# Two blocks of a transformer on one core: the parts of the latent projection in two banks, and two weight splits in other places

## What is computed

```python
h = rms_norm(x, norm_mix_pre[i])
z = h @ w_in[i]
c_q, c_kv, k_rope, q_c, k_c, v_c, g_a, g_b, g_c = jnp.split(z, split_points, axis=-1)
o_a = mla_attention(c_q, c_kv, k_rope, ...)      # latent attention, 8 heads
o_b = fourier_mix(h)
o_c = windowed_gqa(q_c, k_c, v_c, ...)           # 8 heads
merged = (jax.nn.sigmoid(g_a) * (o_a @ w_branch_a[i]) + jax.nn.sigmoid(g_b) * (o_b @ w_branch_b[i])
          + jax.nn.sigmoid(g_c) * (o_c @ w_branch_c[i]))
x = x + rms_norm(merged @ w_out[i], norm_mix_post[i])
h = rms_norm(x, norm_ffn_pre[i])
ff = (jax.nn.silu(h @ w_ffn_gate[i]) * (h @ w_ffn_up[i])) @ w_ffn_down[i]
x = x + rms_norm(ff, norm_ffn_post[i])
e = (p[i] @ w_ple_proj[i]) * jax.nn.sigmoid(x @ w_ple_gate[i])
x = x + rms_norm(e, norm_ple[i])
```

## Time and profile before

| | |
|---|---|
| median of 3 runs | 1958.55 us (1958.01 to 1962.77) |
| the profiled execution | 1960.33 us |
| its span in the trace | 1958.5 us |
| PE busy | 1895.8 us, 97% of the span |
| DVE, ACT, POOL busy | 57%, 49%, 9% |
| place A | 15 to 46 us |
| place B | 478 to 514 us |
| place C | 945 to 970 us |

### The profile page before, as it was taken

The page is one execution under the profiler, slowest core; times in us unless marked ns, Lnnn a source line. Parts: engine busy times, 40 slices in busy tenths (PEclk is TensorE's granted clock), DMA queues, the critical chain, the costliest instruction groups (busy, mean ns, idle before and its releaser), DMA issues.

```text
span 1958.5 us, 26222 instructions
## 1 busy us (share of the span) xinstructions
PE 1895.8 (97%) x9054; PEld 1544.7 (79%) x9054; DVE 1112.5 (57%) x1340; ACT 958.2 (49%) x1256; POOL 169.5 (9%) x262
## 2 busy tenths in 40 slices
PE   8999999999999999999999999899999999989998
PEld 7777888887876888888788887688888888758886
DVE  6565664458566565455744455654565445555544
ACT  5555454445556445444544445544455444555443
POOL 5310010000321001000100012000011000100000
PEclk9999999999999999999999999999999999999999
DMA  6234555554423556555555553365555555435552
GB/s 219 97 110 155 193 193 193 193 193 153 162 65 129 181 175 221 182 184 189 188 184 192 193 185 127 109 209 193 193 187 179 193 193 175 160 107 172 185 183 104
DMA packets 204843, 332.71 MB, mean 170 GB/s; under 512 B 11344, under 2 KB 150224, under 8 KB 204752
## 3 DMA queue, kind: packets, MB, share of 16 engines
q1 hardware_dynamic: 200240, 319.33, 48.3%
q0 software_dynamic: 3120, 11.02, 1.7%
q10 hardware_dynamic: 1392, 1.21, 0.2%
HBM read 330.47 MB, written 1.05 MB: 169 GB/s over the span
## 4 chain that ended last, share of the span: by engine, by line
PE 84%; issue 6%; ACT 4%; DVE 3%; POOL 1%; DMA 1%; ACTq 0%; DVEq 0%; POOLq 0%
PE ps L542 26%; PE ps L554 26%; PE ps L549 26%; PE ps L576 3%; ACT whi L1207 2%; PE ps L720 1%; PE ps L732 1%; PE ps L748 1%; ACT prob L1304 1%; DVE soft L1786 0%; DVE wlo L1659 0%; DMA freq<-freq_dram 0%; DVE prob L1798 0%; DMA gains<-gains_dram 0%; DVE prob L1779 0%
## 5 line engine op out<-in xcount | busy, mean ns | idle before, releaser
L1659 DVE TENSOR_TENSOR wlo<-raw,whi 128x2048 fp32r<-128x2048 f32 (+1 forms) x304 | 686.1, 2257 | 543.0 <-ACT whi L1207 542.5
L1207 ACT ACTIVATE whi<-raw 128x2048 fp32r<-128x2048 f32 (+2 forms) x308 | 581.0, 1886 | 427.4 <-PE ps L554 425.3
L542 PE MATMUL ps<-whi,act_hi 128*128 128x512 f32 (+1 forms) x1632 | 444.7, 393 | 5.4 <-issue 2.1
L549 PE MATMUL ps<-wlo,act_hi 128*128 128x512 f32 (+1 forms) x1632 | 442.3, 389 | 0.0
L554 PE MATMUL ps<-whi,act_lo 128*128 128x512 f32 (+1 forms) x1632 | 435.7, 388 | 0.7 <-DVE act_lo L1665 0.7
L554 PEld LDWEIGHTS ps<-whi,act_lo 128*128 128x128 f32 x1632 | 304.9, 188 | 65.0 <-DVE act_lo L1665 1.6
L549 PEld LDWEIGHTS ps<-wlo,act_hi 128*128 128x128 f32 x1632 | 303.2, 188 | 63.2 <-issue 1.1
L542 PEld LDWEIGHTS ps<-whi,act_hi 128*128 128x128 f32 x1632 | 298.1, 188 | 64.5 <-issue 2.9
L1251 ACT ACTIVATE hid<-ps,stat 128x256 f32<-128x256 f32 x132 | 62.7, 475 | 282.9 <-PE ps L576 197.3
L2214 POOL TENSOR_TENSOR stat<-stat,eps 128x1 f32<-128x1 f32 x44 | 23.0, 522 | 1494.1 <-ACT prob L1238 1493.8
L1711 DVE SCALAR_TENSOR_TENSOR hid<-ps,stat,hid 128x256 f32<-128x256 f32 x132 | 63.5, 481 | 123.1 <-ACT hid L1251 123.1
(11 more groups left out here) (203 smaller groups left out, 1652.4 us busy)
## 6 DMA issues: line engine op xcount, KB each, us to landing
raw<-ffn_w_gate_dram SPq DMA_DIRECT2D x88, 512.0 KB, 4.0
raw<-ffn_w_up_dram SPq DMA_DIRECT2D x88, 512.0 KB, 5.0
raw<-ffn_w_down_dram SPq DMA_DIRECT2D x88, 512.0 KB, 3.9
raw<-w_in_dram SPq DMA_DIRECT2D x64, 512.0 KB, 4.3
raw<-w_ffn_gate_dram SPq DMA_DIRECT2D x44, 512.0 KB, 4.0
raw<-w_ffn_up_dram SPq DMA_DIRECT2D x44, 512.0 KB, 5.0
raw<-w_ffn_down_dram SPq DMA_DIRECT2D x44, 512.0 KB, 3.9
raw<-a_w_qkv_dram SPq DMA_DIRECT2D x24, 512.0 KB, 4.4
```

The costliest lines, as they stand in the source:

```text
L542: nc.tensor.matmul(o, hi, a, start=start and i == 0, stop=False)
L549: nc.tensor.matmul(o, hi, a, start=False, stop=False)
L1207: nc.scalar.activation(whi[:, u % SLOTS, 0:words], raw[:, u % SLOTS, 0:words], ACT.Copy)\
L1659: nc.vector.tensor_tensor(wlo[:, u % SLOTS, 0:words], raw[:, u % SLOTS, 0:words], whi[:, u % SLOTS, 0:words].bitcast(F32), ALU.subtract)\
```

## The change

1. PE's parts of the latent projection take turns in two banks: parts 0 and 2 of tile t in bank 4 + 2t, part 1 in bank 5 + 2t. Part 1 waits for no reader any more, part 2 for the reader of part 0. DVE reads from the bank that belongs to the part.
2. At a layer's end DVE splits unit 2 of the next layer ahead of tile 1's residual (`add_embedded(13, 1)`), not behind it.
3. ACT splits unit 3 at the head of the next layer, ahead of `square_second`, not at the end of the layer before. On the way from the first to the second layer this is the same order with the loop's return ahead of the split. At the second block's start the split comes behind the first `silu` and ahead of `square_second`. At the start of the program it moves into the loop.

```diff
@@ PE, layer1 @@
-                        free_before("half", HF_Z + 2 * c + t)
+                        if c == 0:
+                            free_before("half", HF_Z + t)
+                        elif c == 2:
+                            was_read("half", HF_Z + t)
...
-                                                [([ps[:, 4 + 2 * t, 0:cols]], act_hi[:, 4 * j + k, t * P:(t + 1) * P],
+                                                [([ps[:, 4 + 2 * t + c % 2, 0:cols]], act_hi[:, 4 * j + k, t * P:(t + 1) * P],
@@ ACT, ffn @@
                 silu(gu, 0)
-                if between is None:
-                    split(1)
-                else:
+                split(1)
+                if between is not None:
                     between()
@@ ACT, ahead of the loop @@
             split(1)
             at_start = False
-            split(1)
...
-                done[0] = SLOTS + 1
+                done[0] = SLOTS
@@ DVE, z_half @@
-                    nc.vector.tensor_scalar(zs[:, t, n0:n0 + cols], half_bank(hf)[:, 0:cols], scale_of(w, t), None,
-                                            ALU.mult)\
+                    nc.vector.tensor_scalar(zs[:, t, n0:n0 + cols], half_bank(hf, 2)[:, c % 2 * 512:c % 2 * 512 + cols],
+                                            scale_of(w, t), None, ALU.mult)\
```

More of the change, by code:

```diff
@@ L1512, in _ @@
             at_start = False
-            split(1)
             with act.Fori(0, DEPTH) as li:
                 w.layer = li
-                done[0] = SLOTS + 1
+                done[0] = SLOTS
                 layer1()
-                assert done[0] == UNITS1 + SLOTS + 1, done
+                assert done[0] == UNITS1 + SLOTS, done
             w.layer = None
-            done[0] = SLOTS + 1
+            done[0] = SLOTS
             sq, tn, hf, gu, hv = T, 0, 0, 0, 0
```

## The result

| | before | changed |
|---|---|---|
| median of 20 runs each, us | 1959.6 (1957.09 to 1964.16) | 1963.24 (1958.77 to 1967.22) |
| ratio, 95% interval | | 1.0016 (1.0008 to 1.0023) |
| the profiled execution, its span | 1960.33, 1958.5 | 1964.49, 1962.7 |
| mean granted clock of TensorE in it | 0.994 | 0.992 |

The changed kernel is slower by some 3.6 us. That is less than 0.3%, so "within 0.3%" came true, but the time lies above the range, and the sign is wrong: 1.2 us less were forecast.

A forecast was written before the change was run, and what follows sets the result against it. PE, busy 97% of the span, was taken as the bound. Gains of 0.4, 0.6 and 0.2 us at places A, B and C sum to 1.2, so 1958.55 - 1.2 = 1957.3 us; range 1955.5 to 1960.5.

The forecast's parts named there:

- within 0.3%: Whole kernel: the time stays within 0.3% (5.9 us) of the kernel before; chance 0.97.
- Place A, 0.4: Latent projection near 39 us: with two banks PE's standstill ahead of part 2 goes; 0.4 us won.
- Place B, two banks: Way from first to second layer: PE starts part 1 at 494.23, not 495.36, waiting for neither bank nor unit 2.
- DVE's work until then is the same sum in another order, so its read of part 0 still starts at 494.48: Way from first to second layer: DVE's read and split of unit 3 keep their times; 0.6 us won there.
- The 0.05 for "something that no row shows, such as a longer fetch at a loop's head": Any place: a cause outside the profile's rows decides the result; chance 0.05.
- Place B, ACT: Way from first to second layer: ACT's split of unit 3 ends at 493.9, 0.26 late, hidden by 1.2 us of cover.
- Place B, the gain row: Way from first to second layer: POOL's row lands later, latents' scaling up to 3 us late; taken as 0, at worst 0.8.
- Place C, 0.2: Second block's start: PE restarts 0.77 earlier though POOL's inverse comes 1.0 later, then waits at unit 3; 0.2 us won.
- Rival 2: POOL held up one DVE instruction more at the second block's start, 1.0 us lost there; time 1958.95; chance 0.12.
- The level: Whole kernel: the starting time from which the gain was subtracted, a median of 1958.55 us.

The follow-up runs named there:

- act_only: The kernel before with only ACT's split of unit 3 moved (part 3 of the change); ratio 1.0002 to the kernel before.
- dve_only: The kernel before with only DVE's split of unit 2 moved ahead of the second residual (part 2 of the change); ratio 1.0037 to the kernel before.
- dve_only_unrolled: The kernel before with DVE's split of unit 2 moved ahead of the second residual and DVE's layer loop written out; ratio 1.0002 to the kernel before.
- dve_unrolled: The changed kernel with DVE's loop over the first block's two layers written out; ratio 1.0003 to the kernel before.
- split_between: The changed kernel with DVE's split of unit 2 between the second residual's two instructions; ratio 0.9995 to the kernel before.
- banks_only: The kernel before with only the two banks for the latent projection (part 1 of the change); ratio 0.9997 to the kernel before.
- warm_gap: The changed kernel with 30 short transposes on PE ahead of its wait for unit 3, in both layers; ratio 1.0027 to the kernel before.
- all_unrolled: The changed kernel with the first block's layer loop written out on PE, DVE and ACT; ratio 0.9994 to the kernel before.
- extra_work_unrolled: The changed kernel with two useless DVE products behind tile 1's residual and DVE's layer loop written out; ratio 1.0041 to the kernel before.
- extra_work: The changed kernel with two useless DVE products ahead of the loop's branch, in both layers; ratio 1.0028 to the kernel before.

## Why the prediction was wrong

- *Place A, 0.4*: the number came, the mechanism isn't shown. The standstill of the earlier trace rows is one of that execution: it is absent, with a single bank too, in `act_only`, `dve_only` and `dve_only_unrolled`, where POOL issued the row of gains 2.2 to 2.6 us earlier. The 0.4 is luck.
- *Place B, two banks*: right. Part 1 starts where it was forecast, one group behind part 0.
- *Place B, "DVE's work until then is the same sum in another order, so its read of part 0 still starts at 494.48"*: **this step failed.** The sum of the busy times is the same, but the way back of the loop was no part of it; it had run beside the split at the end of the old order. By the forecast, with PE's 0.33 us of lead at this point (492.99 against 493.32), unit 3 would have started at 497.2; it started at 499.9, 2.7 later. The slow groups, for which the sum had no term, add 2.4 to that (5.28 less 2.73 and the 0.1 of a restart), and the one behind them 0.2 (1.11 instead of 0.91). That is 5.3 or 5.4 us against the forecast, from 0.6 won to 4.8 lost. The other places came out in the size that was forecast, and by the profiled executions the whole error is the same 5.4: the like of the profiled execution should have taken 1959.1 and took 1964.49.
- *The 0.05 for "something that no row shows, such as a longer fetch at a loop's head"*: it was not true that no row showed it. The rows of the branch's line, 491.1 and 494.3, stood in the trace of before. I had counted ACT's way back at the same place (0.92 idle in the earlier trace rows) and not asked the same of DVE, where it was hidden.
- *Place B, ACT*: the way back and the load come ahead of unit 3's split, which ended at 492.25 + 1.92 = 494.17 (493.9 forecast), and DVE took it 3.4 later. No effect. The drain of 1.38 us that the Trainium skill gives behind a table load (ScalarE: Activation LUTs, What ACT_TABLE_LOAD costs) isn't seen here either: the load at 490.95 takes 1.28, and the split starts at 492.25.
- *Place B, the gain row*: in the changed kernel the scalings waited for POOL only; no cost was seen. Where the way back doesn't hold DVE up, they do wait for the row (0.26 us in `dve_unrolled`, 0.34 in `dve_only_unrolled`, 0.88 in `split_between`), and PE has no gap at part 2 from it.
- *Place C, 0.2*: right in mechanism and size. POOL's steps are 2.10 and 1.48 long, PE's gaps 0.78 and 0.35, 0.25 won. The rule of the Trainium skill on VectorE and GpSimd (SBUF — State Buffer, Who interferes with whom) agrees with these rows: the first step ends at 963.50, DVE's split of 961.18 at 963.46. Rival 2, a longer hold, did not come.
- *The level*: 1958.55 was the median of three runs; that of 20 is 1959.6. Of the 5.9 us by which the forecast of 1957.3 missed 1963.24, 1.05 is this.

## What to carry to other kernels

Before an instruction is moved away from the end of a loop's body, look up when the branch behind it is executed and when the body's first instruction comes, on that engine, in the trace. If the time between is longer than the engine's idle time there, the work at the end covers it, and what is moved is not only its own duration. What counts is from where on the sequencer waits for nothing more: a long instruction behind the last wait is cover, the same one ahead of it is none. "The same sum in another order" is true of busy times only.

## What the runs showed of the hardware

**The way back of a long loop takes microseconds.** From the branch to the head of the loop, on DVE: 3.2 us before, 3.77 in the changed kernel, 3.58 in `dve_only`. The nine kernels with this loop have 2.8 (`banks_only`) to 3.9 (`warm_gap`), in one trace each; why it differs is open. PE stood still for 2.1 to 2.6. The number of packets of one of the two queues that carry instructions goes down with the loops. These are the page's lines of that queue (packets, MB, share) in the changed kernel, in `dve_only_unrolled` and in `all_unrolled`:

```profile
q14 instruction: 41, 0.34, 0.0%
```

```profile
q14 instruction: 36, 0.29, 0.0%
```

```profile
q14 instruction: 31, 0.25, 0.0%
```

This fits a fetch of the body's first instructions from memory. That it is the fetch which takes the time, and what sets its length, was not tested on its own. The Trainium skill has the rule (Runtime: NRT & Kernel Launch, Instruction fetch mechanics): a branch taken to a place outside the part of the program that the engine holds has to wait for a fetch. The traces fit it: DVE's 2.8 to 3.9 us stand behind the branch that is taken, and the branch of the same line that isn't taken shows no such time (964.8 to 965.83 in the changed kernel).

**A standstill may cost nearly double**: 3.12 us of idle time and 2.4 more behind it at place B. The medians here depend on how often the clock falls. The runs of each kernel grouped by the mean granted clock of the run (before: the 27 runs beside `dve_only`, so the two columns were not timed side by side; mean us and number of runs):

| mean granted clock | before | changed |
|---|---|---|
| 0.996 | | 1958.8 (1) |
| 0.995 | 1957.1 (6) | 1959.5 (2) |
| 0.994 | 1959.4 (13) | 1961.9 (6) |
| 0.993 | 1961.1 (7) | 1963.3 (3) |
| 0.992 | 1961.8 (1) | 1964.7 (4) |
| 0.991 | | 1965.8 (4) |

At the same clock the changed kernel is 2.2 to 2.9 us slower; one step of 0.001 is some 2 us, and the changed kernel has more runs at the lower steps, which is the rest of the 3.6 us. PE's idle time at the three places grew by 1.3 us only (3.12 less 0.97 at place B, 0.78 + 0.35 less 1.67 at place C, 0.3 less at place A). The step of the clock is too coarse to say where the other 0.9 to 1.6 us at equal clock lie. Length alone doesn't decide whether slow groups follow: they came behind 3.12 us (changed kernel), 2.97 (`dve_only`) and 1.83 (`extra_work_unrolled`, place B), and not behind 2.58 (`extra_work`, place B) or 3.05 (`extra_work_unrolled`, place C), though behind 3.05 in `extra_work`. And every trace, that of before too, has slow stretches in the attention, which the change doesn't touch, at other places from execution to execution (before: rows from 88.9, 166.4, 566.5 and 632.9; the one from 566.5 has only waits of 1.48 and 0.41 us ahead of it). What else decides it stays open. A difference of 2 or 3 us between two single traces can therefore be nothing but this; the reading of place B rests on the standstill and on the ratios, not on the slow groups.
